# Two-block model in one Trainium2 kernel: filler bank emptied ahead of an item's maximum, second weight unit in halves, unused matmuls moved and added at waits

## The chip, the cores and the metric

The kernel runs on one core of a Trainium2 chip. The metric is device time in microseconds for one launch; less is better. Engines are named as in the profile: PE (TensorE matmuls), PEld (its weight loads), DVE (VectorE), ACT (ScalarE), POOL (GpSimd), SP (the queue that issues most DMAs).

## What is computed

Two blocks one after the other on 512 tokens of width 1024, in float32. The first block has a retention layer and a differential-attention layer; the second prepends 16 meta tokens (528 in all), runs a gated feed-forward layer, then latent attention (MLA, 8 heads) and a gated delta rule side by side, then another feed-forward layer. The part on which the change works most is the latent attention:

```python
q = (rmsnorm_2(c_q_raw, q_norm) @ w_uq).reshape(b, length, MLA_HEADS, MLA_NOPE + MLA_ROPE)
kv = (rmsnorm_2(c_kv_raw, kv_norm) @ w_ukv).reshape(b, length, MLA_HEADS, MLA_NOPE + MLA_V)
s = (einsum('bqhd,bkhd->bhqk', qn_b, k_nope) + einsum('bqhd,bkd->bhqk', qr_b, k_rope)) * scale
s = jnp.where(causal, s, -jnp.inf)
p = jax.nn.softmax(s, axis=-1)
return jnp.einsum('bqhk,bkhd->bqhd', p, v)      # per block of 128 queries
...
merged = sigmoid(gate_mla) * y_mla + sigmoid(gate_gdn) * y_gdn
```

## The kernel before

**Weights in units.** All projections read their weights in units of 128 x 2048 values (eight K tiles of 256 columns). SP loads unit u into one of four buffers (`RAW`), ACT rounds it to a high part (`hi`, `hi_part`, L891, into `WH`), POOL subtracts to get the low part (`lo`, `lo_part`, L752, into `WL`), and PE waits for `lo_done` and then does 48 matmuls (`project`): two chunks `m` of 128 output columns, eight K tiles `k` each, three products (high x high, high x low, low x high) of 512 columns. Unit 0, the first of the kernel, already goes in halves: two DMAs, two roundings, two subtractions, and PE waits for the second half only at its fifth K tile. Unit 1 goes whole. On ACT its rounding stands behind the DMA issues of the gain rows (`gain_row`, `other_rows`, L932 to L956).

**Unused matmuls.** `keep_clock(bank, count)` issues `count` 128 x 128 float32 matmuls of a constant into a bank of PS that nobody reads; each shows as two records in the trace. In `project` the argument `warm` places such a run in the third unit of the first key projection (`j_kv_k`), behind the wait for the unit's low part and ahead of the wait for the result slot (`slot_free`).

**Key projection.** Behind `j_kv_k`'s second unit PE spreads the inverse norm (`norm_spread("norm1")`); DVE scales the rope table with it (L1386) and then rotates chunk after chunk (`rotate`: L1530, L1534, L1537). L1530 is what frees a chunk's slot of PS; there are four slots, so chunk n needs that of chunk n - 4.

**Second block, before latent attention.** The projections are `j_cq`, `j_g0`, `j_kvm`, `j_g1` (one unit each), with the sums and spreads of the norms "cq" and "ckv" between them, written out by hand: `norm_sums("cq")` behind `j_kvm`, `spread_cq` (the spread of "cq", then the sums of "ckv") between the two chunks of `j_g1`, `norm_spread("ckv")` behind it. What follows from `norm_spread("cq")` is a chain: DVE L1719, ACT L1172, ACT rounds the unit `j_ukv`, POOL subtracts it and takes the root for "ckv" (L769), ACT writes the diagonal (L919), PE spreads it. Then come the eight chunks of the queries' up-projection (`for n, off in enumerate(...)`, n = 0 to 7; six matmuls each) and those of keys and values. ACT copies chunks 4 to 7 and all of the keys and values out (L1179 to L1194), in order, without a pause once chunk 7 is there.

**Latent attention.** 32 items (head h, query block b) go through a loop of steps on each engine, s = 0 to 44. In step s PE computes the scores of item s (behind a wait for the exponentials of item s - 2), transposes the exponentials of item s - 2, and multiplies those of item s - 3 with the values. DVE takes the maximum of item s (L1766, or L1769 for the longest), ACT the exponential (L1206). Between these PE puts **fillers**: matmuls of three gate units (`j_gm`), 24 to a chunk, 2 behind the scores and 3 behind the transposes (`mla_fill`), all into bank 1 of PS. When a chunk's 24th is done DVE must empty the bank (`gate_out`, L1689: multiply into a stage, which SP then stores to memory) before the first filler of the next chunk may start (`mfill_free`). Six chunks are filled; the fillers of a chunk end in step 4, 10, 15, 21, 26 or 32. On DVE the emptying stands in the step after that, behind the maximum of that step's item:

```python
for s in range(HEADS * NT + MLA_LAG):
    if s < HEADS * NT:
        dve.wait_ge(ma_s, s + 1)            # scores of item s
        nc.vector.tensor_reduce(NEGM2[...], PS[...], AX.X, ALU.max, negate=True).then_inc(ma_max, 1)
    while mla_kept < mla_filled[s]:
        dve.wait_ge(done, j_gm.tick0 + mla_kept + 1)
        gate_out(4 + mla_kept, PS[:, 1, :]).then_inc(mfill_free, 1)
        mla_kept += 1
```

Of the kernel before, what the change touches and what calls it, by code (L numbers as in the profile page):

```python
# [4 lines left out]
F32 = mybir.dt.float32  # L5
# [6 lines left out]
KC = D // P  # L12
# [58 lines left out]
def build(nc, A, out):  # L71
    ctx = ExitStack()
    with ctx:
        def sem(name):
            return ctx.enter_context(nc.semaphore(name))
# [140 lines left out]
        hi_done, lo_done = sem("w_hi_done"), sem("w_lo_done")  # L216
        done = sem("pe_done")
# [354 lines left out]
        def _(sp):  # L572
# [8 lines left out]
            def load(jb, src):  # L581
                for n in range(jb.units):
                    u = jb.unit0 + n
                    if u == 0:
                        continue
                    if u >= RAWS:
                        sp.wait_ge(done, unit_ticks[u - RAWS])
                    src(n // 4, n % 4, RAW[:, u % RAWS, :], raw_in[u % RAWS])
                    if u == 1:
                        sp.dma_start(TAB[:, :, :], c_rope_ret).then_inc(s_tab, 16)  # L590
                        for n, name in enumerate(("lam_q1", "lam_q2", "lam_k1", "lam_k2")):
                            sp.dma_start(LAMV[:, n, :], A[name]).then_inc(s_lamv, 16)
# [144 lines left out]
        def _(pool):  # L737
# [43 lines left out]
            lo(1)  # L781
# [103 lines left out]
        def _(act):  # L885
# [71 lines left out]
            hi(1)  # L957
# [389 lines left out]
        def _(dve):  # L1347
# [409 lines left out]
            for s in range(HEADS * NT + MLA_LAG):  # L1757
                if s < HEADS * NT:
# [12 lines left out]
                while mla_kept < mla_filled[s]:  # L1771
                    dve.wait_ge(done, j_gm.tick0 + mla_kept + 1)
                    gate_out(4 + mla_kept, PS[:, 1, :]).then_inc(mfill_free, 1)
                    mla_kept += 1
# [303 lines left out]
        def _(pe):  # L2078
# [4 lines left out]
            def project(jb, xh, xl, cols, kc=KC, k_ready=None, after=None, last_k=None, units=None, second=None, between=None, at_chunk=None,  # L2083
# [3 lines left out]
                def body(i, j):  # L2087
# [4 lines left out]
                    if u:  # L2092
                        pe.wait_ge(lo_done, u + 2)
# [30 lines left out]
                    for m, k in order:  # L2124
# [5 lines left out]
                        if warm is not None and (n, m, k) == (2, 0, 0):  # L2130
                            keep_clock(*warm)
# [192 lines left out]
            project(j_kv_k, UH, UL, SEQ_COLS, k_ready=(ul_done, applied["norm1"]), after="norm1", warm=(idle_bank, 17))  # L2324
# [82 lines left out]
            project(j_kvm, UH, UL, ALL_COLS)  # L2407
            norm_sums("cq")

            def spread_cq():  # L2410
                norm_spread("cq")
                norm_sums("ckv")
# [10 lines left out]
            for n, off in enumerate((512, 768, 640, 896, 0, 128, 256, 384)):  # L2423
                c = j_uq.chunk0 + n
# [395 lines left out]
```

## Time and profile before

| | us |
|---|---|
| median of three runs | 2129.03 (2127.67 to 2131.23) |
| the profiled execution, whole | 2131.52 |
| its span, first to last instruction | 2129.7 |
| PE busy in it | 2062.0 (97%) |
| DVE, ACT, POOL busy | 815.4, 736.3, 778.8 |
| mean granted TensorE clock, share of full | 0.990 |

The profiled execution is 1.8 us longer than its span, and 2.5 us above the median. A timeline row gives the start, the duration, the engine, the line, the operation with output and inputs, the shape and the number of instructions; what stands in brackets is how long the engine had sat idle before it, and what ended that. A row of the windows has the busy time of each engine in a stretch and, third from the end, the granted clock: 1.00 is 2.4 GHz, 0.50 is 1.2 GHz.

### The profile page before, as it was taken

What the parts mean: (1) busy time and instruction counts of PE and PEld (TensorE: products, weight loads), DVE (VectorE), ACT (ScalarE), POOL (GpSimd) and SP (SyncE); (2) the same over time, 40 slices, a digit from 0 to 9 for tenths busy, and PEclk for the clock granted to TensorE, in tenths of its full rate; (3) what the DMA queues carried; (4) which work ended last, traced back from release to release, by engine and by line L of the source; (5) the groups of instructions that cost most, each with busy time, mean ns of one, the idle gap of its engine ahead of it and who ended that gap; (6) DMA issues with size and microseconds to landing.
All of it is one profiled execution on the core that took longest, in us unless ns stands there. A gap on an engine that the chain in (4) does not pass through costs nothing.

```text
span 2129.7 us, 32015 instructions
## 1 busy us (share of the span) xinstructions
PE 2062.0 (97%) x13924; PEld 1768.5 (83%) x13924; DVE 815.4 (38%) x1284; ACT 736.3 (35%) x1139; POOL 778.8 (37%) x246
## 2 busy tenths in 40 slices
PE   7999999999999999999999989999999999999998
PEld 6899888878977789999999867798777788888886
DVE  3400675145357655220222241256566544211222
ACT  5423222336556544221222353342222333212222
POOL 4443332545322154334433421035244235334432
PEclk9999999999999999999999999999999999999999
DMA  5223122222210122223322430031113133223322
GB/s 172 90 89 112 52 75 79 79 89 80 94 59 28 40 79 80 80 75 106 98 72 88 101 99 30 31 96 60 42 61 111 62 98 99 87 77 114 99 65 74
DMA packets 170036, 171.52 MB, mean 81 GB/s; under 512 B 16924, under 2 KB 160664, under 8 KB 169896
## 3 DMA queue, kind: packets, MB, share of 16 engines
q1 hardware_dynamic: 168492, 167.25, 24.9%
q8 instruction: 110, 1.80, 0.4%
q10 hardware_dynamic: 1404, 2.23, 0.3%
q14 instruction: 30, 0.25, 0.0%
HBM read 163.17 MB, written 6.29 MB: 80 GB/s over the span
## 4 chain that ended last, share of the span: by engine, by line
PE 88%; DVE 5%; issue 3%; ACT 2%; POOL 1%; DMA 1%; ACTq 0%; SPq 0%; DVEq 0%; POOLq 0%
PE ps L2080 86%; PE ps L2082 2%; DVE coef L1575 1%; POOL w_lo L752 1%; ACT w_hi L891 0%; ACT diag L919 0%; DMA x_rows<-in_x 0%; DVE gdn_x L1945 0%; DVE u_lo L1392 0%; POOL stat L769 0%; DVE tmp L1404 0%; DVE neg_max L1563 0%; DVE gdn_inv_t L1928 0%; ACT u_hi L945 0%; DVE mla_q L1748 0%
## 5 line engine op out<-in xcount | busy, mean ns | idle before, releaser
L752 POOL TENSOR_TENSOR w_lo<-w_raw,w_hi 128x2048 fp32r<-128x2048 f32 (+3 forms) x157 | 674.6, 4299 | 942.2 <-ACT w_hi L891 936.7
L2080 PE MATMUL ps<-u_hi,w_hi 128*128 128x512 f32 (+1 forms) x1904 | 585.6, 347 | 19.1 <-POOL w_lo L752 5.7
L2080 PE MATMUL ps<-u_hi,w_lo 128*128 128x512 f32 (+1 forms) x1904 | 580.4, 345 | 0.0
L2080 PE MATMUL ps<-u_lo,w_hi 128*128 128x512 f32 (+1 forms) x1904 | 571.0, 345 | 1.1 <-DVE u_lo L1392 0.8
L2080 PEld LDWEIGHTS ps<-u_hi,w_hi 128*128 128x128 f32 x1904 | 329.7, 189 | 62.8 <-issue 10.4
L2080 PEld LDWEIGHTS ps<-u_lo,w_hi 128*128 128x128 f32 x1904 | 327.2, 189 | 44.1 <-DVE u_lo L1392 5.5
L2080 PEld LDWEIGHTS ps<-u_hi,w_lo 128*128 128x128 f32 x1904 | 329.2, 189 | 40.3 <-issue 0.5
L891 ACT ACTIVATE w_hi<-w_raw 128x2048 fp32r<-128x2048 f32 (+3 forms) x157 | 279.9, 1784 | 178.2 <-PE ps L2080 168.9
L2080 PE MATMUL ps<-hidden_hi,w_hi 128*128 128x264 f32 (+1 forms) x528 | 141.1, 321 | 0.0
L2080 PE MATMUL ps<-hidden_lo,w_hi 128*128 128x264 f32 (+1 forms) x528 | 141.0, 322 | 0.0
L2080 PE MATMUL ps<-hidden_hi,w_lo 128*128 128x264 f32 (+1 forms) x528 | 140.8, 321 | 0.0
L2080 PE MATMUL ps<-w_lo,u_hi 128*128 128x256 f32 x384 | 107.9, 281 | 0.0
L2080 PE MATMUL ps<-w_hi,u_lo 128*128 128x256 f32 x384 | 107.9, 281 | 0.0
L2080 PE MATMUL ps<-w_hi,u_hi 128*128 128x256 f32 x384 | 107.6, 280 | 0.0
L1667 DVE SCALAR_TENSOR_TENSOR residual<-ps,residual 128x528 f32<-128x528 f32 (+1 forms) x32 | 22.4, 700 | 209.8 <-PE ps L2080 209.8
L1644 DVE TENSOR_TENSOR tmp<-sg,ps 128x528 f32<-128x528 f32 (+1 forms) x44 | 30.5, 696 | 172.6 <-PE ps L2080 172.5
L2080 PEld LDWEIGHTS ps<-hidden_lo,w_hi 128*128 128x128 f32 x528 | 87.7, 188 | 8.1
L2080 PEld LDWEIGHTS ps<-hidden_hi,w_hi 128*128 128x128 f32 x528 | 87.4, 188 | 7.9
L2080 PEld LDWEIGHTS ps<-hidden_hi,w_lo 128*128 128x128 f32 x528 | 87.6, 188 | 7.7
L1641 DVE TENSOR_TENSOR sg<-ps,rstd_row 128x528 f32<-128x528 f32 (+1 forms) x44 | 30.4, 699 | 165.3 <-PE ps L2080 165.2
L1130 ACT ACTIVATE hidden_hi<-tmp 128x528 fp32r<-128x528 f32 (+1 forms) x44 | 28.2, 642 | 175.7 <-DVE tmp L1644 175.7
L1128 ACT ACTIVATE sg<-sg 128x528 f32<-128x528 f32 (+1 forms) x44 | 28.0, 641 | 170.6 <-DVE sg L1641 170.6
(376 smaller groups left out, 2948.0 us busy)
## 6 DMA issues: line engine op xcount, KB each, us to landing
w_raw<-in_w_in_a SPq DMA_DIRECT2D x23, 1024.0 KB, 5.2
w_raw<-in_ffn_w_gate SPq DMA_DIRECT2D x22, 1024.0 KB, 5.3
w_raw<-in_ffn_w_up SPq DMA_DIRECT2D x22, 1024.0 KB, 5.3
w_raw<-in_w_in SPq DMA_DIRECT2D x17, 1024.0 KB, 5.4
w_raw<-in_ffn_w_down SPq DMA_DIRECT2D x16, 768.0 KB, 4.4
w_raw<-in_ffn_w_down SPq DMA_DIRECT2D x16, 640.0 KB, 4.2
w_raw<-in_w_out_a SPq DMA_DIRECT2D x8, 1024.0 KB, 5.2
w_raw<-in_w_kv SPq DMA_DIRECT2D x8, 1024.0 KB, 5.4
```

The source lines that it names most:

```text
L752: pool.tensor_tensor(WL[:, u % RAWS, part], RAW[:, u % RAWS, part], WH[:, u % SPLITS, part].bitcast(F32), ALU.subtract).then_inc(lo_done, 1)
L891: nc.scalar.activation(WH[:, u % SPLITS, part], RAW[:, u % RAWS, part], ACT.Copy).then_inc(hi_done, 1)
L1128: nc.scalar.activation(SG[:, m, 0:width], SG[:, m, 0:width], ACT.Silu).then_inc(silu_done, 1)
L1130: nc.scalar.activation(HH[:, 4 * i + 2 * (j // 2) + m, 0:width], TMP[:, m, 0:width], ACT.Copy).then_inc(hh_done, 1)
L1575: nc.vector.scalar_tensor_tensor(out=COEF[:, 0:1], in0=ESUM[:, g % 2, 0:1], scalar=RSUM[:, h % 3, b, 1:2], in1=LAMS[:, 5:6], op0=ALU.mult, ...
L1641: nc.vector.tensor_tensor(halves(SG[:, m, 0:width]), acc(slot, width), halves(RSTDB[:, 0:width]), ALU.mult).then_inc(ps_free[slot], 1)
L1644: nc.vector.tensor_tensor(halves(TMP[:, m, 0:width]), halves(SG[:, m, 0:width]), acc(slot, width), ALU.mult).then_inc(ps_free[slot], 1)
L1667: nc.vector.scalar_tensor_tensor(out=halves(RES[:, k, cols]), in0=acc(slot, width), scalar=0.5, in1=halves(RES[:, k, cols]), op0=ALU.mult, ...
L2080: return nc.tensor.matmul(o, a, b, start=start, stop=stop, **kw)
L2082: return nc.tensor.transpose(o, x, IDENT[0:n, 0:n])
```

## The change

Four edits.

1. **Second weight unit in halves.** Unit 1 is loaded by two DMAs (`raw_half`, `raw_in[1]`), rounded by two instructions on ACT and subtracted by two on POOL. PE waits for the first half (`lo_half`) and for the second at the fifth K tile of the first chunk. Ahead of that first wait it issues 11 unused matmuls into bank 3.
2. **Filler bank.** On DVE the `while` that empties the filler bank now stands at the head of the step, ahead of the wait for the item's scores and of its maximum.
3. **Key projection.** The unused matmuls of `warm` go ahead of the wait for the third unit's low part, and are 15 instead of 17.
4. **Unused matmuls at other waits.** 8 ahead of `norm_sums("cq")`, 7 ahead of `norm_spread("cq")` in `spread_cq`, 10 ahead of chunk 6 of the queries' up-projection.

```diff
@@ SP, load
-                    src(n // 4, n % 4, RAW[:, u % RAWS, :], raw_in[u % RAWS])
+                    if u == 1:
+                        for a, landed in enumerate((raw_half, raw_in[u])):
+                            sp.dma_start(RAW[:, u, a * UNIT // 2:(a + 1) * UNIT // 2].rearrange("p (c n) -> p c n", c=KC // 2),
+                                         w_in_a[:, a * KC // 2:(a + 1) * KC // 2, UCOL:2 * UCOL]).then_inc(landed, 16)
+                    else:
+                        src(n // 4, n % 4, RAW[:, u % RAWS, :], raw_in[u % RAWS])
@@ POOL
-            lo(1)
+            pool.wait_ge(hi_half, 1)
+            pool.tensor_tensor(WL[:, 1, 0:UNIT // 2], RAW[:, 1, 0:UNIT // 2], WH[:, 1, 0:UNIT // 2].bitcast(F32),
+                               ALU.subtract).then_inc(lo_half, 1)
+            lo_part(1, slice(UNIT // 2, UNIT), 3)
@@ ACT
-            hi(1)
+            act.wait_ge(raw_half, 16)
+            nc.scalar.activation(WH[:, 1, 0:UNIT // 2], RAW[:, 1, 0:UNIT // 2], ACT.Copy).then_inc(hi_half, 1)
+            hi_part(1, slice(UNIT // 2, UNIT), raw_in[1])
@@ DVE, latent attention
             for s in range(HEADS * NT + MLA_LAG):
+                while mla_kept < mla_filled[s]:
+                    dve.wait_ge(done, j_gm.tick0 + mla_kept + 1)
+                    gate_out(4 + mla_kept, PS[:, 1, :]).then_inc(mfill_free, 1)
+                    mla_kept += 1
                 if s < HEADS * NT:
...
-                while mla_kept < mla_filled[s]:
-                    dve.wait_ge(done, j_gm.tick0 + mla_kept + 1)
-                    gate_out(4 + mla_kept, PS[:, 1, :]).then_inc(mfill_free, 1)
-                    mla_kept += 1
@@ PE, project
-                    if u:
+                    if warm is not None and n == 2:
+                        keep_clock(*warm)
+                    if u == 1:
+                        keep_clock(3, 11)
+                        pe.wait_ge(lo_half, 1)
+                    elif u:
                         pe.wait_ge(lo_done, u + 2)
...
-                        if warm is not None and (n, m, k) == (2, 0, 0):
-                            keep_clock(*warm)
+                        if u == 1 and (m, k) == (0, KC // 2):
+                            pe.wait_ge(lo_done, u + 2)
@@ PE, order written out
-            project(j_kv_k, ..., after="norm1", warm=(idle_bank, 17))
+            project(j_kv_k, ..., after="norm1", warm=(idle_bank, 15))
...
             project(j_kvm, UH, UL, ALL_COLS)
+            keep_clock(3, 8)
             norm_sums("cq")
 
             def spread_cq():
+                keep_clock(3, 7)
                 norm_spread("cq")
                 norm_sums("ckv")
...
             for n, off in enumerate((512, 768, 640, 896, 0, 128, 256, 384)):
+                if n == 6:
+                    keep_clock(7, 10)
```

## Rows read from the trace of the kernel before

**Rows 1.** The page: busy time of each engine.
```profile
PE 2062.0 (97%) x13924; PEld 1768.5 (83%) x13924; DVE 815.4 (38%) x1284; ACT 736.3 (35%) x1139; POOL 778.8 (37%) x246
```

**Rows 2.** Waits of PE: us in total, times, longest.
```profile
PE ps L2080 <- DVE gate_stage L1689: 5.5, 5, 1.5
```

**Rows 3.** Windows with the granted clock at 0.50 (third from the end).
```profile
29.70:36.40 6.70, 3.25 (x8) 2.58 (x9) 0.00 (x0) 4.89 (x6) 6.70 (x2) 0.50 0.34 121
1241.40:1248.10 6.70, 6.63 (x16) 5.19 (x17) 1.60 (x3) 2.45 (x2) 1.05 (x1) 0.50 0.39 136
1302.90:1306.20 3.30, 3.30 (x12) 2.51 (x11) 0.14 (x1) 1.85 (x2) 0.00 (x0) 0.50 0.49 186
1343.80:1347.10 3.30, 3.30 (x14) 2.73 (x13) 0.00 (x0) 2.18 (x2) 0.07 (x1) 0.50 0.37 143
1364.30:1371.00 6.70, 6.70 (x23) 5.51 (x23) 0.56 (x2) 1.38 (x4) 0.00 (x0) 0.50 0.00 0
```

**Rows 4.** Timeline of the start: halves of unit 0, unit 1 whole, PE behind it.
```profile
12.44 1.05 ACT L891 ACTIVATE w_hi<-w_raw 128x1024 fp32r<-128x1024 f32 x1
13.66 2.35 POOL L752 TENSOR_TENSOR w_lo<-w_raw,w_hi 128x1024 fp32r<-128x1024 f32 x1 [12.10 <-ACT w_hi L891]
...
26.59 3.71 ACT L891 ACTIVATE w_hi<-w_raw 128x2048 fp32r<-128x2048 f32 x2 [3.53 <-issue]
28.59 13.57 POOL L752 TENSOR_TENSOR w_lo<-w_raw,w_hi 128x2048 fp32r<-128x2048 f32 x3 [7.01 <-ACT w_hi L891]
33.15 0.79 PE L2080 MATMUL ps<-u_hi,w_hi 128*128 128x512 f32 x1 [5.67 <-POOL w_lo L752]
```

**Rows 5.** Timeline: twelve unused matmuls (24 records) at the full clock.
```profile
453.85 2.84 PE L2080 MATMUL ps<-ident,ones 128*128 128x128 f32 x24
```

**Rows 6.** Timeline of the key projection, third unit: PE, and DVE freeing slots.
```profile
485.78 5.69 PE L2080 MATMUL ps<-ident,ones 128*128 128x128 f32 x34 [2.55 <-POOL w_lo L752]
486.80 0.68 DVE L1530 SCALAR_TENSOR_TENSOR tmp<-ps,diff_rope 128x512 f32<-128x512 f32 x1
...
493.08 0.68 DVE L1530 SCALAR_TENSOR_TENSOR tmp<-ps,diff_rope 128x512 f32<-128x512 f32 x1
```

**Rows 7.** Timeline of PE in latent attention: the scores of six heads' first items.
```profile
1290.42 0.51 PE L2080 MATMUL ps<-mla_k,mla_q 96*128 96x144 f32 x2
...
1306.38 0.51 PE L2080 MATMUL ps<-mla_k,mla_q 96*128 96x144 f32 x2
...
1320.59 0.51 PE L2080 MATMUL ps<-mla_k,mla_q 96*128 96x144 f32 x2
...
1334.76 0.51 PE L2080 MATMUL ps<-mla_k,mla_q 96*128 96x144 f32 x2
...
1351.27 0.51 PE L2080 MATMUL ps<-mla_k,mla_q 96*128 96x144 f32 x2
...
1366.53 0.85 PE L2080 MATMUL ps<-mla_k,mla_q 96*128 96x144 f32 x2
```

**Rows 8.** Timeline around the second emptying of the filler bank.
```profile
1297.93 0.49 PE L2080 MATMUL ps<-u_hi,w_lo 128*128 128x512 f32 x1
...
1301.19 0.71 DVE L1769 TENSOR_REDUCE neg_max<-ps 128x1 f32<-128x528 f32 x1 [2.40 <-PE ps L2080]
1301.81 0.68 DVE L1689 TENSOR_TENSOR gate_stage<-ps,rstd_row 128x512 f32<-128x512 f32 x1
...
1302.64 0.61 PE L2080 MATMUL ps<-u_hi,w_hi 128*128 128x512 f32 x1 [1.49 <-DVE gate_stage L1689]
```

**Rows 9.** Timeline of PE at the three places of edit 4 and the spread of "ckv".
```profile
1225.20 1.05 PE L2080 MATMUL ps<-ones,sumsq 128*128 128x1 f32 x8 [1.93 <-DVE sumsq L1356]
...
1231.78 1.02 PE L2080 MATMUL ps<-diag,ones 128*128 128x512 f32 x2
...
1241.47 2.10 PE L2080 MATMUL ps<-diag,ones 88*128 88x264 f32 x4 [2.14 <-ACT diag L919]
...
1255.20 0.50 PE L2080 MATMUL ps<-cq_hi,w_hi 128*128 128x512 f32 x1 [1.06 <-DVE tmp L1740]
```

More of the change, by code:

```diff
@@ L216, in build @@
         hi_done, lo_done = sem("w_hi_done"), sem("w_lo_done")
+        raw_half, hi_half, lo_half = sem("w_half_in"), sem("w_hi_half_done"), sem("w_lo_half_done")
         done = sem("pe_done")
@@ L2323, in _ @@
             keep_clock(idle_bank, 12)
-            project(j_kv_k, UH, UL, SEQ_COLS, k_ready=(ul_done, applied["norm1"]), after="norm1", warm=(idle_bank, 17))
+            project(j_kv_k, UH, UL, SEQ_COLS, k_ready=(ul_done, applied["norm1"]), after="norm1", warm=(idle_bank, 15))
             pe.wait_ge(lam_step, 3)
```

## Prediction, made before the changed kernel was run

> **What bounds the kernel now.** I read the page first: PE is busy for 97% of the span [rows 1], so only two things can move the time: the little that PE waits, and the clock at which it runs. So I read PE's list of waits and then asked for the granted clock microsecond by microsecond. The clock was full except in seven stretches. Five of them bear on this change [rows 3]: one behind the wait for unit 1, one behind the wait for the spread of "ckv", and three in latent attention. A sixth lies inside the unused matmuls of the key projection, whose 34 records took 5.69 us [rows 6] where 34 at the full rate would take 34 x 0.118 = 4.0 (24 took 2.84 [rows 5]). The seventh, behind the end of latent attention, the change doesn't touch. In each stretch the reader is to see a PE that is busy at 1.2 GHz, so that about half of its time there is lost. Ahead of each PE had idled: 5.67 us [rows 4], 2.55 us [rows 6], 2.14 us [rows 9], and in latent attention the wait for the filler bank to be emptied, five times, 5.5 us in all and 1.5 at most [rows 2]. The slow stretches follow the three longer of these five waits (1.49, 1.36 and 1.16 us by the timeline); the two short ones (0.80 and 0.65) and the 1.93 us of rows 9 were followed by none. So a wait here costs itself and, mostly, half of a slow stretch.
>
> **Edit 1, unit 1 in halves.** Before: ACT starts at 26.59 (until then it issues DMAs, so the unit has long landed and an extra DMA issue on SP isn't felt), POOL at 28.59, PE at 33.15 [rows 4]. After: the first half's rounding takes 1.05 and its subtraction 2.35 us, as for unit 0 [rows 4], so with the gaps between engines of 0.1 it is ready at 26.59 + 1.05 + 0.1 + 2.35 + 0.1 = 30.2. The second half ends 2.4 later, at 32.6; PE reaches it after 12 matmuls of 0.233 us, at 33.0, and doesn't wait. (0.233: 24 matmuls lie between the sums' end at about 1226.2 and 1231.78 [rows 9].) The 11 unused matmuls are 22 records, 22 x 0.118 = 2.6 us, from 27.3 to 29.9: they end before the half is there and cost nothing. Gain: 33.15 - 30.2 = 2.95, and the slow clock from 33.15 to 36.4, half of 3.3 us [rows 3], 1.6. Together **4.5 us**. Of what is queued behind on ACT and POOL, unit 2's parts come 0.3 us later or earlier, with 5 us to spare. If the unused matmuls don't hold the clock, only 2.95 is left.
>
> **Edit 3, key projection.** PE is free at 483.1 (2.55 and a little before 485.78 [rows 6]). The 30 records now start there, 30 x 0.118 = 3.5 us, end at 486.7, and the low part is there since 485.8. What comes last then is the slot: DVE's L1530 ends at 486.80 + 0.68 = 487.5 [rows 6], and it hangs on POOL and DVE work that doesn't move. Before, the first real matmul came at 491.3; that would be 3.7 us of gain. But the next chunk needs the slot that DVE frees at 493.08 + 0.68 = 493.76 [rows 6], and 24 matmuls from 487.5 end at 493.1: a new wait of 0.6 us. Gain **3.0 us** with the slow stretch in it; in an execution whose clock hadn't fallen there, 4.0 instead of 5.7 us of unused matmuls, it is 1.4. I take 3.0, since I compare with this execution.
>
> **Edit 2, filler bank.** The last filler of a chunk ends at 1297.93 + 0.49 = 1298.4; the emptying takes 0.68 [rows 8] and would be over by 1299.5, behind the previous maximum. Where it now stands, DVE first takes the maximum of an item whose scores are ready only at 1301.2, and empties the bank from 1301.81 to 1302.49; PE waits 1.49 us [rows 8]. Moved ahead it is done 1.7 us before that maximum can start, so the maximum isn't delayed. What is queued behind it on DVE is that maximum, and behind that ACT's exponential; both keep their time. `gate_out` also waits for a store of its stage, which was issued a whole chunk (20 us) earlier. So all five waits go, 5.5 us [rows 2]. The clock: from one head's first scores to the next PE takes 15.96, 14.21, 14.17, 16.51 and 15.26 us [rows 7], with 16, 19, 18, 16 and 17 fillers by the program. The third has one wait of 0.65 and no slow clock, 13.52 without it; at 0.233 a filler the others should take 13.05 (16) and 13.29 (17). The excess is 2.91 + 3.46 + 1.97 = 8.34 us for heads one, four and five. The slow clock runs on until 1371.0 [rows 3], 4.5 us into the head after, half of which is 2.2. With the waits of 0.80 and 0.65 in sound heads that is 12.0 us. Against it stands a new wait: in one step with three fillers only, the product with the values would come 0.3 us ahead of DVE's norm. Gain **11.7 us**. Its lower bound is the waits alone, 5.2; nothing in the rows lets it go below zero unless the maximum is held back (below).
>
> **Edit 4, three runs of unused matmuls.** (a) 8 ahead of `norm_sums("cq")`: 16 x 0.118 = 1.9 us in a wait of 1.93 [rows 9]: nothing (at half the clock, 1.9 us lost). (b) 7 ahead of `norm_spread("cq")`: PE doesn't wait there; the row at 1231.78 has no bracket [rows 9]. 14 x 0.118 = 1.65 us of work are added, and everything up to the spread of "ckv" is a chain from `norm_spread("cq")`, so the wait of 2.14 us that follows isn't filled but moved: **1.65 us lost**. (c) 10 ahead of chunk 6: 20 x 0.118 = 2.36 in a wait of 1.06 [rows 9]. The surplus is 1.3, less the 0.15 us that the wait takes to be seen; ACT's copies run without a pause from chunk 7 to the start of attention, so nothing absorbs it: **1.15 us lost**. Bounds for (b) and (c) together: 0 if a wait absorbs them, 2 x 2.8 = 5.6 lost if the clock is at half there (it was until 1248.1 [rows 3]). I take 2.8, the rate of rows 5, since PE was at the full clock at both places. The slow stretch from 1241.4 stays, since nothing fills the wait ahead of it; the range of that is 2.6 us either way.
>
> **The sum.** 4.5 + 3.0 + 11.7 - 2.8 = 16.4 us, from the profiled execution's 2131.5: 2115.1. Its own time is 2.5 us above the median of 2129.0. The executions must differ in how often the clock falls, as no other engine is near the path; the changed kernel has two slow stretches left instead of seven, so it should gain a little less against the median than against this execution. Median less sum would be 2112.6, profiled execution less sum 2115.1; I take **2114**.
>
> **Rivals.** (1) The clock falls in latent attention from thin work, not from the waits: scores, transposes and products of 64 columns load PE little, and with all shifted the stretches only move. For it: the seventh stretch followed waits of 0.7 us only. Against it: from 1248.1 to 1302.9 and from 1306.2 to 1343.8, with the same thin work and no wait there over 1.5 us, the clock held until the wait of 1.49 and that of 1.36 came [rows 3, 8]. Then edit 2 is worth 11.7 - (12.0 - 5.5) = 5.2 and the time is 2120.5. Chance 0.16. "TensorE: Matmul & The Clock Gate" of the Trainium skill, in its section "HAM oscillation — how this bites in real kernels", warns of idle gaps longer than all but the first of those above; by that rule the waits of 1.2 to 1.5 us can't be the cause, and this rival would be the case. The trace speaks against the rule, with slow stretches right behind three such waits. (2) The unused matmuls of edit 4 cost nothing or pay, since in other executions the clock fell behind the 1.93 us wait: 2.8 us better, 2111. Chance 0.2. (3) The wait moves on: without the filler wait PE waits for the exponentials of item s - 2 (maximum 0.7, exponential 0.9, both behind ACT's rounding of a unit of 1.9). They have a whole step of 3.3 us or more; if they came last at all five places, 5 us would come back: 2119. Chance 0.06. (4) Slower: DVE's emptying, now in front of the maximum, waits for its stage's store, and maximum, exponential and PE stop with it. The store is issued a chunk earlier and would have to take over 13 us to be felt; it turns the sum only if it holds each of the five up by more than 3.3 us. At 5 us each the time is 2139. Chance 0.02. (5) The halves of unit 1 or the moved run do nothing for the clock: 2118. Chance 0.04. The forecast case has 0.52.
>
> **Range and chances.** The forecast has 2110.5 to 2117.5 by itself (a slow stretch more or less is 1.6 to 3.3 us). Down to 2108 it takes in (2), up to 2121 (1), (3) and (5). Outside are (4) and the tails of the other cases, together about 0.18. Faster by over 0.2% (4.3 us, what a measurement of this kernel can tell from no change): 0.95; within 0.2%: 0.03; slower: 0.02.
>
> **What would show it.** Right: PE without a wait for `gate_stage` L1689, and no clock of 0.50 between the start of attention and its end; PE's first matmul of unit 1 at 30.2; the first real matmul of the third key unit near 487.5, a wait of 0.6 us one chunk later; 14 records of unused matmuls at 1231.78 less the shift of 7.5, the wait for "ckv" still 2.1 us. Wrong: a bracket before the fillers or before the transposes in attention, DVE idle in front of L1689 waiting for a store, slow stretches there in spite of a busy PE, or a shorter wait for "ckv".

## The result, and the profile after

| | before | after |
|---|---|---|
| median, first comparison (6 runs each) | 2130.06 us | 2114.55 us (2113.71 to 2118.18) |
| ratio, with its 95% interval | | 0.9929 (0.9918 to 0.9941) |
| profiled execution, whole | 2131.52 | 2114.54 |
| its span | 2129.7 | 2112.4 |

The changed kernel is 15.1 us faster by the ratio (12.6 to 17.5), forecast 2114. Later it was run again, six times, beside its relatives: 2116.26, ratio 0.9931. The sum was right; two of its terms weren't, and their errors nearly cancelled, which is luck. That is what the experiments showed, and the traces of one execution each did not.

The page, engines, to be read against [rows 1]:

```profile
PE 2057.6 (97%) x13992; PEld 1767.3 (84%) x13992; DVE 822.4 (39%) x1284; ACT 736.1 (35%) x1140; POOL 779.5 (37%) x247
```

PE has 68 records more (the unused matmuls) and is busy 4.4 us less: unused work was added, and slow clock went. PE's waits no longer have a row for `gate_stage` [rows 2]. What has come in its place in latent attention is small (of the 0.6 us for `mla_norm` below 0.2 stood there before); the wait for the diagonals is still there, and the lines that the change shifted are L1797 for the head's norm, L1751 for the rotation of the queries, L928 for the diagonal, L1541 for the keys' rotation:

```profile
PE ps L2091 <- ACT diag L928: 3.5, 4, 2.1
PE ps L2091 <- DVE tmp L1751: 1.0, 1, 1.0
PE ps L2091 <- DVE mla_norm L1797: 0.6, 2, 0.4
PE ps L2091 <- DVE tmp L1541: 0.5, 1, 0.5
```

The timeline of the start, against [rows 4]: POOL's first half of unit 1, PE's unused matmuls, and PE's first matmul of the unit. Columns are start, duration, instruction, and in brackets the idle time and what ended it:

```profile
27.73 2.37 POOL L788 TENSOR_TENSOR w_lo<-w_raw,w_hi 128x1024 fp32r<-128x1024 f32 x1 [6.16 <-ACT w_hi L967]
...
27.32 2.62 PE L2091 MATMUL ps<-ident,ones 128*128 128x128 f32 x22
30.15 0.50 PE L2091 MATMUL ps<-u_hi,w_hi 128*128 128x512 f32 x1 [0.21 <-POOL w_lo L788]
```

30.15 was forecast as 30.2. (A bracket `<-issue` means that the profile shows nothing that the engine waited for.) The key projection, third unit, against [rows 6]: the unused matmuls, the first real one, and the new wait a chunk later.

```profile
479.15 3.51 PE L2091 MATMUL ps<-ident,ones 128*128 128x128 f32 x30
483.69 0.47 PE L2091 MATMUL ps<-u_hi,w_hi 128*128 128x512 f32 x1 [1.02 <-issue]
...
489.96 0.50 PE L2091 MATMUL ps<-u_hi,w_hi 128*128 128x512 f32 x1 [0.46 <-DVE tmp L1541]
```

483.69 is the forecast 487.5 less the 4 us that edit 1 has already won.

The three places of edit 4 and the spread of "ckv", against [rows 9]:

```profile
1218.47 1.95 PE L2091 MATMUL ps<-ident,ones 128*128 128x128 f32 x16
1220.56 1.05 PE L2091 MATMUL ps<-ones,sumsq 128*128 128x1 f32 x8
...
1227.15 1.72 PE L2091 MATMUL ps<-ident,ones 128*128 128x128 f32 x14
1228.71 1.02 PE L2091 MATMUL ps<-diag,ones 128*128 128x512 f32 x2
...
1238.40 1.13 PE L2091 MATMUL ps<-diag,ones 88*128 88x264 f32 x4 [2.12 <-ACT diag L928]
...
1247.80 2.39 PE L2091 MATMUL ps<-ident,ones 128*128 128x128 f32 x20
1251.20 0.51 PE L2091 MATMUL ps<-cq_hi,w_hi 128*128 128x512 f32 x1 [1.00 <-DVE tmp L1751]
```

The reader sees three things. The first run fills its wait: the sums have no bracket. The 14 records of the second stand right ahead of the spread, and the wait for "ckv" is as long as before (2.12). And behind the third run PE still waits 1.00 us for DVE's rotation.

Second emptying of the bank, now ahead of the maximum, against [rows 8]:

```profile
1293.17 0.57 DVE L1781 TENSOR_REDUCE neg_max<-ps 128x1 f32<-128x400 f32 x1 [3.33 <-PE ps L2091]
1293.66 0.68 DVE L1700 TENSOR_TENSOR gate_stage<-ps,rstd_row 128x512 f32<-128x512 f32 x1
...
1295.85 0.48 PE L2091 MATMUL ps<-u_hi,w_hi 128*128 128x512 f32 x1
1296.13 0.71 DVE L1784 TENSOR_REDUCE neg_max<-ps 128x1 f32<-128x528 f32 x1 [1.79 <-PE ps L2091]
```

The filler at 1295.85 has no bracket, and the maximum behind the emptying still waits for PE (1.79 us), not for the emptying.

The clock in windows (length, PE busy with the number of instructions, granted clock of PE, share of the DMA engines, GB/s), against [rows 3]:

```profile
810.50:813.90 3.40, 3.40 (x18) 0.51 0.00 0
1241.40:1248.10 6.70, 6.70 (x32) 1.00 0.00 0
1373.70:1377.10 3.40, 3.40 (x20) 0.51 0.06 20
1262.00:1371.00 109.00, 107.38 (x635) 1.00 0.16 45
```

All of latent attention runs at the full clock (the last row). But there is a slow stretch at 810.5 that the trace of before doesn't have, and 1241 is at the full clock although nothing fills the wait ahead of it. So which stretches an execution has is partly chance. One of before and one of after can't settle what each edit is worth, and the prediction had been made from one.

**Where the time went, in these two traces.** The same PE matmul starts earlier by: 4.4 us in unit 1 (36.30 to 31.90), 3.95 at 211, 7.5 at the key unit, 6.9 a chunk later, 4.7 at 929 (the new slow stretch took 1.6 of it, and 0.6 more goes in three steps of 0.2 by 925, whose cause no row shows), 3.1 at the spread of "cq" (1231.78 to 1228.71), 4.0 at the start of latent attention, 16.2 at its end, 17.3 at the end of the kernel. (The 6.7 us of slow clock that before has behind the spread of "ckv" cost it 3.0 us on the way, but only 0.9 of that is left at chunk 6, where both traces wait for DVE.)

### The profile page after: what moved, and what is told of

The parts are those of the page before. It is cut to its first block, busy times and chain, and to the rows that moved or that the text cites. A ratio compares the mean times of both kernels' runs of the same rounds, so it can differ in the third digit from the quotient of the medians.

```text
span 2112.4 us, 32155 instructions
## 1 busy us (share of the span) xinstructions
PE 2057.6 (97%) x13992; PEld 1767.3 (84%) x13992; DVE 822.4 (39%) x1284; ACT 736.1 (35%) x1140; POOL 779.5 (37%) x247
## 4 chain that ended last, share of the span: by engine, by line
PE 87%; DVE 6%; issue 3%; ACT 2%; POOL 1%; DMA 1%; ACTq 0%; SPq 0%; DVEq 0%; POOLq 0%
PE ps L2091 85%; PE ps L2093 2%; DVE coef L1586 1%; POOL residual L781 1%; DMA x_rows<-in_x 0%; DVE sumsq L1367 0%; ACT diag L928 0%; DVE u_lo L1403 0%; DVE mla_q L1759 0%; DVE gdn_x L1956 0%; DVE tmp L1415 0%; DVE neg_max L1574 0%; DVE gdn_inv_t L1939 0%; POOL w_lo L758 0%; POOL stat L775 0%
```

## The experiments

All medians are of 6 to 12 executions; those of before beside them are 2129.28 for edit 2 alone, the filled waits, the first kernel without edit 4 and the moved 7; 2129.56 for the two parts of edit 1, edit 3 and the end of latent attention; 2130.08 for the other four. Beside each time stands the number of us by the ratio of the runs, with its 95% interval, negative for faster than before.

### Edit 2 alone

```diff
             for s in range(HEADS * NT + MLA_LAG):
+                while mla_kept < mla_filled[s]:          # emptying, moved ahead of the maximum
+                    ...
                 if s < HEADS * NT:
                     ...
-                while mla_kept < mla_filled[s]:
-                    ...
```

> The kernel before with edit 2 alone: the filler bank emptied ahead of the item's maximum. The theory of the prediction (the waits of 1.2 to 1.5 us make the clock fall behind them, so that edit 2 takes away the waits, 5.5 us, and the slow stretches behind them, 6.6 us) expects 11.7 us less than the kernel before: about 2118.4 against 2130.1, no wait for gate_stage and no granted clock of 0.50 between 1270 and 1365. Rival 1 (thin work makes the clock fall, the waits don't) expects the waits gone and slow stretches still inside latent attention: 5.2 us less, about 2124.9.

Measured: 2124.08, ratio 0.9967, -7.0 us (-9.4 to -4.5). The medians differ by 5.2, rival 1's price, and the interval leaves out 11.7. Yet the trace has what the forecast's mechanism asks for, no wait of PE for `gate_stage` (5.5 us before) and a full clock from the first score to the last product:

```profile
1267.00:1377.20 110.20, 108.60 (x641) 1.00 0.16 46
1379.00:1385.00 6.00, 5.52 (x29) 0.50 0.11 40
```

The trace bears out the mechanism and the medians don't bear out its price. The mean granted clocks don't either. Take span x (1 - clock) as the time lost to the clock (it counts slow stretches in which PE waits as well, and clocks are given in steps of 0.001, 2 us of span): the eight executions lose 17.0 us on the average, the nineteen of before beside them 16.8, with a standard error of 0.9 for the difference. So in the runs edit 2 shows its waits, and no less slow clock. What is needed is how long latent attention takes in more executions of the old order, and three of the later kernels keep that order.

### The waits kept, but filled

```diff
+                def freed(c):                             # ahead of each wait for the bank
+                    if c:
+                        ...                               # a bank that the next transposes overwrite
+                        for _ in range(5):
+                            mm(PS[:, 4 + no % 2, 0:P], ONES[:, :], IDENT[:, :])
+                    wait(pe, mfill_free, c)
```

> The kernel before, with the bank still emptied behind the maximum, and 5 unused matmuls (10 records, 1.2 us at full rate) ahead of each of the five waits for it. The waits stay as long as they are but PE works through them: at 0.65 and 0.80 us the run is longer than the wait by 0.9 us together. The theory that idle time ahead of it makes the clock fall expects no slow stretch in latent attention, and the end of it earlier by 6.6 - 0.9 = 5.7 us: about 2124.4. Rival 1 (thin work, not idle time) expects slow stretches as before: 2130.1 + 0.9 = 2131.0.

Measured: 2126.26, -3.0 us (-4.7 to -1.1). The longest wait is now 10 unused records and a short rest:

```profile
1302.24 1.28 PE L2080 MATMUL ps<-ident,ones 128*128 128x128 f32 x10
1303.80 0.51 PE L2080 MATMUL ps<-u_hi,w_hi 128*128 128x512 f32 x1 [0.28 <-DVE gate_stage L1689]
```

No real work became shorter, so 3.0 us can only come from the clock, and the mean granted clocks say the same: 13.8 us lost here, 16.8 in before. The rival's 2131.0 is outside. But it is half of the expected 5.7.

### Edit 1 in its two halves

Unit 1 in halves, without unused matmuls:

```diff
+                    if u == 1:
+                        pe.wait_ge(lo_half, 1)
-                    if u:
+                    elif u:
                         pe.wait_ge(lo_done, u + 2)
```

> The kernel before with unit 1 of the weights split in halves and no unused matmuls ahead of it. PE starts the unit at 30.2 instead of 33.15 and a wait of 2.7 us remains in front of it. The theory that idle time makes the clock fall expects the slow stretch there to stay, as in the three profiles that have the undivided unit: a gain of 2.9 us only, and the later wait at 43 takes some 0.4 of it back (about 2127.0 against 2129.5). The rival (the long wait of 5.7 us was needed, one of 2.7 isn't enough) expects no slow stretch and 2.9 + 1.6 us: about 2125.0. In this kernel the fillers of latent attention still wait for their bank, so its profile also shows once more how many slow stretches such an execution has there: by the prediction's pricing four (13.6 us), by the medians of the kernel with edit 2 alone about none or one.

Measured: 2125.29, -4.0 us (-6.4 to -1.9). In the trace the unit starts at 30.23 behind a wait of 2.67, and the clock is down for all PE work from there to 33.3:

```profile
30.23 0.80 PE L2091 MATMUL ps<-u_hi,w_hi 128*128 128x512 f32 x1 [2.67 <-POOL w_lo L788]
...
30.10:33.30 3.20, 3.07 (x7) 0.50 0.64 227
```

So the halves bring the 2.9 us and a wait of 2.7 costs the slow stretch, as the theory said; the rival (2.7 is too short) fell in the trace. The medians can't tell 2.9 from 4.5.

The unused matmuls, without the halves:

```diff
+                    if u == 1:
+                        keep_clock(3, 23)
                     if u:
                         pe.wait_ge(lo_done, u + 2)
```

> The kernel before with the undivided unit 1 and 23 unused matmuls (46 records, 5.4 us) in PE's wait of 5.7 us ahead of it. Expected by the theory: PE starts the unit at 33.1 as before, at full clock, and the slow stretch of 6.8 us behind it, 3.3 us of which are work of PE, is gone: 1.6 us (about 2127.9 against 2129.5). Rival (the slow stretch is set by the matmuls behind the wait, not by the idle time): the stretch from about 30 to 37 stays and nothing is gained. Latent attention is unchanged here too; its slow stretches are counted as in the kernel with the halves.

Measured: 2128.45, ratio 1.0004, +0.9 us (-1.7 to +3.2). The trace shows the step itself, a full clock from 27.5 to 40:

```profile
27.36 5.30 PE L2080 MATMUL ps<-ident,ones 128*128 128x128 f32 x46
33.22 0.50 PE L2080 MATMUL ps<-u_hi,w_hi 128*128 128x512 f32 x1 [0.56 <-POOL w_lo L752]
...
27.50:40.00 12.50, 11.94 (x75) 1.00 0.26 84
```

PE's matmuls from 36.6 on come 1.4 us earlier than in the trace of before. The runs neither confirm nor exclude so little.

### Edit 3 alone

```diff
-                        if warm is not None and (n, m, k) == (2, 0, 0):   # behind the wait for the low part
-                            keep_clock(*warm)
+                    if warm is not None and n == 2:                       # ahead of it
+                        keep_clock(*warm)
-... warm=(idle_bank, 17)
+... warm=(idle_bank, 15)
```

> The kernel before with edit 3 alone: 15 unused matmuls ahead of the wait for the key unit instead of 17 behind it. The prediction's price is 3.0 us (about 2126.5 against 2129.5) where the clock had fallen in the 17, and 1.4 us (2128.1) in an execution where it hadn't. Two profiles of three with the old order show that slow stretch (at 487), so the median should show about 2.5: 2127.0. The first real matmul of the unit at about 487.9 instead of 491.2, and a wait of 0.5 us one chunk later. Latent attention is unchanged; its slow stretches are counted.

Measured: 2127.08, ratio 0.999, -2.1 us (-4.5 to +0.2); the medians differ by 2.5. The trace has the first real matmul at 488.19 and the wait of 0.49 a chunk later; the shift against before is 3.0 us at both, since there the clock had fallen.

### How long latent attention takes

These kernels keep the old order there, so their traces give three more executions of it. First scores of the first item, and the transposes of the last norm, for before, edit 3 alone, halves alone, unused matmuls alone:

```profile
1267.23 0.48 PE L2080 MATMUL ps<-mla_k,mla_q 96*128 96x144 f32 x2 [1.02 <-ACT mla_v L1194]
1388.28 1.09 PE L2082 MATMUL ps<-ident,mla_norm 128*128 128x128 f32 x4 [0.67 <-DVE mla_norm L1786]
```

```profile
1268.99 0.48 PE L2080 MATMUL ps<-mla_k,mla_q 96*128 96x144 f32 x2 [1.10 <-ACT mla_v L1194]
1383.71 0.63 PE L2082 MATMUL ps<-ident,mla_norm 128*128 128x128 f32 x4 [0.66 <-DVE mla_norm L1786]
```

```profile
1268.59 0.48 PE L2091 MATMUL ps<-mla_k,mla_q 96*128 96x144 f32 x2 [1.01 <-ACT mla_v L1205]
1383.33 0.63 PE L2093 MATMUL ps<-ident,mla_norm 128*128 128x128 f32 x4 [0.67 <-DVE mla_norm L1797]
```

```profile
1269.60 0.48 PE L2080 MATMUL ps<-mla_k,mla_q 96*128 96x144 f32 x2 [1.00 <-ACT mla_v L1194]
1385.97 0.63 PE L2082 MATMUL ps<-ident,mla_norm 128*128 128x128 f32 x4 [0.67 <-DVE mla_norm L1786]
```

That is 121.05, 114.72, 114.74 and 116.37 us. All four have the same five waits, 5.5 us. (With these waits filled it is 114.80, no slow stretch either.) The slow stretches in them are four of 3.4 us (one pair back to back, 6.8), none, none and one. The changed kernel:

```profile
1263.24 0.48 PE L2091 MATMUL ps<-mla_k,mla_q 96*128 96x144 f32 x2 [1.03 <-ACT mla_v L1205]
1372.12 0.63 PE L2093 MATMUL ps<-ident,mla_norm 128*128 128x128 f32 x4 [0.67 <-DVE mla_norm L1797]
```

108.88, and in all nine traces with the new order 108.9 or 109.0, with no slow stretch ahead of the last wait. So edit 2 is worth 5.8 us plus 1.6 for each slow stretch that the execution would have had: 12.2 against the profiled execution of before, 7.8 against the mean of the four (116.7). The 7.0 (4.5 to 9.4) of edit 2 alone agrees with the second; so would the waits alone, and the mean clocks above fit those better. How many slow stretches edit 2 saves in a usual execution is not settled.

### Edit 4 taken out, in whole and in part

The changed kernel without its three runs:

```diff
-            keep_clock(3, 8)
             norm_sums("cq")
             def spread_cq():
-                keep_clock(3, 7)
                 norm_spread("cq")
...
-                if n == 6:
-                    keep_clock(7, 10)
```

> The changed kernel without the three runs of unused matmuls around the latent norms (8, 7 and 10 of them). The theory from the two traces: the 7 cost what they take, 1.6 us, the 8 and the 10 lie in waits and cost nothing, so this is 1.6 us faster than the changed kernel: 2113.0. Rival 2 (the runs pay, since they hold the clock behind waits of 1.9, 2.1 and 1.0 us): without them up to three more slow stretches of 3.4 us come between 1215 and 1260, 1.7 us each: 2113.0 + 1.7 to 5.1, so 2114.7 to 2118.1.

Measured: 2116.28, ratio 0.9935, where the changed kernel had 2114.55 in the comparison before it. The difference was too small for runs in different comparisons, so both were run again side by side:

> The changed kernel once more, beside its relatives on one chip: about 2114.6 median, 2113.7 to 2118.2. What is asked is its distance to the kernel without edit 4 (below), which was 1.7 us of median with runs on different chips, and whether its profile again has one slow stretch or none between 1215 and 1260 and none inside latent attention.

> The changed kernel without the three runs of unused matmuls of edit 4, once more. The prediction priced edit 4 at 2.8 us lost, so this would be 2111.8 beside 2114.6. The reading of the first run (the unused work costs 1.6 to 4 us, the slow stretches that it prevents around 1208 to 1245 cost 3 to 5 us more) expects 2116.0 here, with two or three slow stretches of 3.4 us between 1205 and 1260, against none or one in the changed kernel.

Measured: 2116.26 with edit 4, 2116.01 without. Over both rounds the medians of twelve runs are 2115.9 with it and 2116.3 without. Edit 4 as a whole changes nothing that can be told here; the 2.8 us of loss didn't come, and neither did the gain that the first run had suggested. By the mean granted clocks the twelve executions with edit 4 lose 9.3 us, those without 12.7 (side by side 10.9 and 12.3). So the unused work costs something and gives about as much back. The traces say where. The table has, for all fourteen, the time from the first spread ahead of this stage (1208.64 in before, 1203.99 in the changed kernel) to the spread of "cq", and from there to the first scores; (a), (b) and (c) are the 8, the 7 and the 10, or the places where they would stand:

| trace | to "cq" | to the scores | slow clock in the stage |
|---|---|---|---|
| without (a), (b), (c): before, waits filled | 23.1 | 35.4 | 6.8 us behind "ckv" |
| without: halves alone, unused matmuls alone, second without edit 4 | 23.1 | 36.5 to 36.9 | 3.4 behind "ckv", 3.4 at (c) |
| without: edit 3 alone, edit 2 alone | 24.7 | 34.5 | 3.4 at (a), 3.4 behind "ckv" |
| without: first without edit 4 | 26.2 | 34.5 | 3.4 at 1208, 3.4 at (a), 3.4 behind "ckv" |
| with all three: changed, end filled | 24.7 | 34.5 | none |
| with all three: changed again | 24.7 | 34.8 | 3.4 behind "ckv" |
| (a), (c): without the 7 | 23.1 | 36.4 | 6.8 behind "ckv" |
| (a), (c), 8 ahead of the "ckv" spread: the 7 moved | 23.1 | 34.5 | none |
| the same, 14 at (c): everything filled | 24.7 | 34.5 | 3.4 at 1209 |

The mean of the whole stage is 59.5 us in the eight traces without edit 4 and 59.3 in the three with it. (b) costs 1.57. A slow stretch at (a) costs 1.55 and came in three of eight; one at (c) costs 2.0 to 2.4 (36.5 to 36.9 against 34.5) and came in three of eight.

Without the 7 only:

```diff
             def spread_cq():
-                keep_clock(3, 7)
                 norm_spread("cq")
```

> The changed kernel without the 7 unused matmuls ahead of the spread of cq, the other two runs kept. If the 7 only add work to a chain (1.65 us by the prediction, 1.57 by the two traces) this is 2113.0 beside 2114.6. If they keep the clock up in front of the wait of 2.1 us for ckv that follows, a slow stretch comes behind that wait in more of the executions and takes it back: 2114.6 or more.

Measured: 2113.63 (2111.51 to 2115.66), ratio 0.9919 (0.9904 to 0.9933), 2.6 us below the changed kernel beside it. That is the fastest kernel of the study by median, though its interval overlaps the changed kernel's. The three kernels that ran side by side fit the table: 2116.01 with none of the runs, 2113.63 with the 8 and the 10, 2116.26 with all three. The trace of the one without the 7 has the slow stretch behind the wait for "ckv", for 6.8 us, and pays for it: 36.4 us from the spread of "cq" to the scores instead of 34.5, of which 0.9 is also in the two traces with this stretch and without the 10 (35.4), and 0.9 comes from the 10, which now end at 1251.5, behind DVE's rotation (1250.3):

```profile
1236.66 2.10 PE L2091 MATMUL ps<-diag,ones 88*128 88x264 f32 x4 [2.14 <-ACT diag L928]
...
1249.15 2.39 PE L2091 MATMUL ps<-ident,ones 128*128 128x128 f32 x20
```

So the 7 cost 1.57 us in the traces (1.65 forecast), and in this one execution the slow clock took the gain back by the start of latent attention (1263.35, and 1263.24 in the changed kernel).

The 7 moved into the wait for "ckv":

```diff
-                keep_clock(3, 7)
...
+            keep_clock(7, 8)
             pe.wait_ge(t_done, 2)
             norm_spread("ckv")
```

> The changed kernel with its 7 unused matmuls ahead of the spread of cq taken out, and 8 put ahead of the wait for the spread of ckv (16 records, 1.9 us in a wait of 2.1 us). The theory expects the 1.6 us back and the clock full behind that wait: 2113.0, or 2111.9 where the changed kernel's executions mostly had a slow stretch there. A rival (the shorter path into the spread of cq only makes PE wait longer elsewhere, since DVE's rotation of the queries ends last ahead of latent attention) expects no more than 0.3 us: 2114.3, with the wait in front of the key chunks longer than 1.0 us.

Measured: 2115.41, ratio 0.9933. The wait shrinks to 0.34 and the clock stays up:

```profile
1235.99 1.95 PE L2091 MATMUL ps<-ident,ones 128*128 128x128 f32 x16
1238.28 1.13 PE L2091 MATMUL ps<-diag,ones 88*128 88x264 f32 x4 [0.34 <-ACT diag L928]
...
1247.68 2.39 PE L2091 MATMUL ps<-ident,ones 128*128 128x128 f32 x20
1251.06 0.50 PE L2091 MATMUL ps<-cq_hi,w_hi 128*128 128x512 f32 x1 [0.99 <-DVE tmp L1751]
```

PE reaches chunk 6 at 1251.06, and at 1251.20 in the changed kernel, but this execution had come into the stage 1.5 us later (a slow stretch at 723). From the stage's first spread to the scores it takes 57.6 us, the shortest of all, 1.6 less than the changed kernel and 1.9 less than the kernel without the 7. So the theory's 1.6 us are there; the rival's wait longer than 1.0 is not (0.99), since DVE's rotation hangs on the spread of "cq" and moves with it. Why the median is 1.8 us above that of the kernel without the 7 stays open: the two were run in different comparisons.

### The waits at the end of latent attention

```diff
+                        if 2 * g + 2 == HEADS:
+                            keep_clock(4 + no % 2, 3)
                         pe.wait_ge(ma_on, 2 * g + 2)
...
+            pe.wait_ge(ma_pt, len(mla_turns) - 1)
+            keep_clock(4 + len(mla_turns) % 2, 3)
             pe.wait_ge(ma_pt, len(mla_turns))
```

> The changed kernel with 3 unused matmuls in each of the two waits at the end of latent attention (0.67 us for the last norm, 0.69 for the copy of its transposes). Every profile so far has a slow stretch of 3.4 to 6.8 us behind them. The theory that these waits make the clock fall expects none there and up to 2.5 us less than the changed kernel, 2112 to 2113. Rival 1 (thin work, here 40 matmuls of 64 columns and transposes without a filler between them, makes the clock fall) expects the stretch to stay and the unused matmuls to cost 0.1 us: 2114.6.

Measured: 2115.44 (2110.94 to 2117.22), ratio 0.993. The two waits (0.67 and 0.69) are filled, and the 28 us behind them are at the full clock:

```profile
1372.25 0.94 PE L2091 MATMUL ps<-ident,ones 128*128 128x128 f32 x6
1373.02 0.60 PE L2093 MATMUL ps<-ident,mla_norm 128*128 128x128 f32 x4
1373.46 0.83 PE L2091 MATMUL ps<-ident,ones 128*128 128x128 f32 x6
...
1372.00:1400.00 28.00, 27.98 (x234) 1.00 0.22 70
```

Of the twelve traces without this filling eleven have a slow stretch right there; of the two with it (this one and the next) none has. The thin matmuls ahead of it are the same. From the last norm's transposes to the kernel's end this trace takes 738.7 us, the twelve without the filling 740.2 to 741.5, so it is worth 1.5 to 2.8 in an execution. The medians don't show it.

Everything filled (8 ahead of the spread of "ckv", 14 instead of 10 ahead of chunk 6, 3 and 3 at the end, no 7):

```diff
-                keep_clock(3, 7)
...
+            keep_clock(7, 8)
...
-                    keep_clock(7, 10)
+                    keep_clock(7, 14)
```

> The changed kernel with the 7 moved into the wait for ckv (8 of them), 14 instead of 10 ahead of chunk 6, which still left a wait of 1.0 us, and 3 in each of the two waits at the end of latent attention. If waits make the clock fall, each of these removes one stretch in part of the executions: lost time by the clock 1 to 2 us below that of the changed kernel and a median of 2112 to 2114. If the sum of waits and unused work is all that counts, it is the changed kernel's 2114.6.

Measured: 2114.9, ratio 0.9925 (0.9911 to 0.994), the changed kernel's time. Its time lost to the clock is 7.7 us, and 10.9 in the changed kernel beside it (but 7.7 in that kernel's first six executions too). Its trace has slow stretches at 1209 and 1663, where the others mostly have none.

## Why the prediction was right

**Edit 1 (4.5 forecast).** Held, in each number that a trace can show: 30.15 for 30.2, 2.62 us of unused records for 2.6, no clock of 0.50. By the traces 4.4 at once and 3.95 by 211, since something ahead of the retention takes 0.4 back that the sum didn't have. The two parts behave as argued: halves alone keep the slow clock, unused matmuls alone remove it. The stretch stands behind the wait in all five traces in which it isn't filled, and in none of nine in which it is. The times of the two parts, by the ratios 4.0 us less and 0.9 more, can't tell 2.95 from 1.6.

**Edit 3 (3.0).** Held: 0.46 for the wait of 0.6, and 3.0 us by the traces. Alone it measured 2.1 to 2.5, between the 3.0 and the 1.4 that the prediction gave for an execution whose clock hadn't fallen. Edits 1 and 3 together, as the kernel without edit 4 against edit 2 alone, are 6.8 us by the ratios and 7.8 by the medians; the sum had 7.5.

**Edit 2 (11.7).** The mechanism was right for the waits, the term too large. The waits went (5.5 forecast), and the new wait for DVE's norm came, as 0.41 us for 0.3 (a second one, of 0.18, stood there before). In the traces the whole is 5.8 us, some 0.7 more than these rows add up to; no row names the rest. The mis-sized term is the slow clock, 6.6 us. The step that failed is "The executions must differ in how often the clock falls, as no other engine is near the path; the changed kernel has two slow stretches left instead of seven, so it should gain a little less against the median than against this execution." The direction was seen and the size wasn't: of four executions of the old order the profiled one has four stretches in latent attention, the others none, none and one. The mean of the four is 1.25 stretches, some 2 us. The runs would have even less: 7.0 less 5.8 leaves 1.2, and the mean clocks show no gain at all.

**Edit 4 (2.8 lost).** (b), the 7, held: 1.57 us in the traces (the shift falls from 4.65 to 3.08), 2.6 by the medians. (c) was mis-sized. The wait of 1.06 ahead of chunk 6 in [rows 9] was short because PE had just gone through 6.7 us of slow clock [rows 3]. The other trace with that much has 1.09; the six with a single stretch of 3.4 there have 1.68 to 2.59:

```profile
1252.22 0.50 PE L2091 MATMUL ps<-cq_hi,w_hi 128*128 128x512 f32 x1 [2.12 <-DVE tmp L1751]
```

(this row is from the second kernel without edit 4). In the changed kernel, with no slow stretch, the 20 records, 2.4 us, and 1.00 of wait fit there. So the 10 cost what the prediction said only behind 6.7 us of slow clock (0.9 in the kernel without the 7, 1.15 forecast); in the changed kernel's two traces they cost nothing or 0.2. And (a) and (c) pay: of the eight traces without them three have a slow stretch at 1225 to 1228, behind the wait that (a) fills, and three at 1253 to 1256, behind the wait that (c) fills; the six traces with them have none at either place. Each by itself could be chance in so few traces; the twelve places filled and sixteen unfilled together (none and six) make that unlikely.

```profile
1253.20:1256.40 3.20, 3.20 (x9) 0.50 0.02 5
```

(This window is from the second kernel without edit 4.) That is rival 2, chance 0.2, in the form that the edit costs nothing: by the rates above the 8 and the 10 pay an estimated 1.4 us on the average (3/8 of 1.55, 3/8 of 2.2), the 7 cost 1.57.

**The sum.** Forecast 4.5 + 3.0 + 11.7 - 2.8 = 16.4. Measured, each by its own runs: edits 1 and 3 about 7, edit 2 7.0, edit 4 about 0: 14, beside 15.1 (12.6 to 17.5) for the whole. The two errors, 4.7 too much for edit 2 and 2.8 too little for edit 4, cancel to 2, by luck, and the forecast stood between the two starting points that it named, 2.5 us apart. Had only edit 4 been seen rightly, the forecast would have been 2111; had only edit 2 been, about 2119. The range held both.

**The rivals.** Rival 1 (thin work, not waits) has its price in the medians of edit 2, and still fell as a mechanism: nine traces pass through the same thin work with no slow stretch, where two of the four with the waits have some. Filled waits have no stretch behind them: at the start five of five traces unfilled and none of nine filled, at "ckv" ten of twelve and none of two, at the end of latent attention eleven of twelve and none of two. What did not fall is the rival's outcome, that the stretches only move: the mean clocks of edit 2 alone are those of before, and of its eight executions one has a trace. "TensorE: Matmul & The Clock Gate" of the Trainium skill, in "HAM oscillation — how this bites in real kernels", blames only idle gaps that are longer than any of the waits of 0.7 to 2.7 us. The traces here contradict it: the granted clock was 0.50 behind the wait of 2.67 in the halves alone and behind the 0.67 and 0.69 at the end of latent attention. The next section of it in the Trainium skill, "A second HAM failure mode: psum-queue depth-cycling", has micro-idles between groups of matmuls as another way for the clock to fall, and that is nearer to what the end of latent attention shows. Rivals 3 to 5 did not occur: the waits for the exponentials didn't move up, no store held the emptying, and the halves with the moved run kept the clock.

**What the sum left out.** The clock of before has an eighth slow stretch, the last 4 us of the kernel, in every trace; it doesn't bear on the change.

**Still open.** Why a wait is followed by a slow stretch in one execution and not in the next. ("TensorE: Matmul & The Clock Gate" of the Trainium skill, in "Part 1: The HAM clock gate", calls the number of slow matmuls at a kernel's start run-variable; no run here takes that further.) The stretch at 810 to 816, behind the norm of the feed-forward, is in twelve of fourteen traces, and one of the two that lack it is the trace of before: the sum had nothing for it, and it took 1.6 us of the changed kernel's gain by the traces. No experiment filled the wait of 1.60 us ahead of it.

## What to carry to other kernels

A slow stretch of the clock in one profile is a sample, not a cost: price it by how often it comes in several executions (kernels that differ elsewhere serve as well), and take only the wait itself for certain. Unused matmuls belong into a wait that the trace shows; ahead of a chain without a wait they cost their length, and where another engine ends last they are free only as long as PE still gets there first. Before two traces are compared at one place, take the time from a common point shortly ahead, or a slow stretch long before is read as the work of the edit. And before a wait is taken as so long, look whether a slow clock just ahead of it has shortened it.

## What the runs showed of the hardware

- The granted clock fell to 0.50 behind waits of PE as short as 0.67 and 0.69 us, 0.6 us of transposes apart, in eleven of twelve traces; with both filled, in none of two.
- It did not fall behind five waits of 0.65 to 1.49 us in two traces of four, and four stretches of it came in one. The wait of 2.1 us for "ckv" was followed by no slow clock in one execution of the changed kernel and by 3.4 us in the other, and by 6.8 us in three others; 6.8 us there put off the start of latent attention by 0.9 us, with 20 unused records behind it by 1.9.
- The runs of the kernel before spread from 2125.75 to 2137.48 us, and their mean granted clocks go along: 0.994 at 2125.75, 0.989 at 2134.76. Span x (1 - clock) is 13 us for the one and 23 for the other, as much as the whole difference of 9.
